# TensorE's four hardware loops written out as straight code, in a two-layer hybrid streaming encoder

## The reference

```
for layer in (0, 1):
    x += mixer(rmsnorm(x))             # layer 0: RG-LRU + sliding-window attention; layer 1: mLSTM
    h  = rmsnorm(x) @ ffn_w_in         # 1024 -> 2 * 2816
    x += (silu(h[:, :2816]) * h[:, 2816:]) @ ffn_w_out
    x += sigmoid(x @ ple_w_gate) * (p[layer] @ ple_w_proj)
y = rmsnorm(x)
```

## Time and profile before

| | |
|---|---|
| median of 3 runs | 2937.79 us (2936.8 to 2938.09) |
| the profiled execution's own time | 2937.61 us |
| its span | 2935.8 us |
| PE busy | 2762.8 us, 94% |
| PEld busy | 2692.7 us, 92% |
| DVE, POOL, ACT busy | 1270.1, 939.1, 603.6 us |
| share of PE in the chain that ended last | 87% |
| TensorE's granted clock, mean | 0.97 |

### The profile page before, as it was taken

How to read it: one execution, slowest core, us unless ns; L and a number is a source line. 1 busy time by engine, 2 the same in 40 slices (tenths; PEclk the granted TensorE clock), 3 DMA queues, 4 the chain that set the end, 5 groups by cost and what they waited for, 6 DMA issues and landing times.

```text
span 2935.8 us, 44303 instructions
## 1 busy us (share of the span) xinstructions
PE 2762.8 (94%) x17273; PEld 2692.7 (92%) x17273; DVE 1270.1 (43%) x2070; ACT 603.6 (21%) x1319; POOL 939.1 (32%) x439
## 2 busy tenths in 40 slices
PE   7999998999999999996999998789999999999996
PEld 5898888999999999996999987688999999999996
DVE  7835474323222223466834036647233332322465
ACT  4524322000000000133122135412100000000042
POOL 3222042333333333432434320023343333333430
PEclk9999999999999999998999999999999999999998
DMA  3101111111111111111212221311111111111111
GB/s 134 32 29 47 42 59 43 44 44 44 44 44 44 44 44 44 53 49 66 81 48 90 90 89 43 131 58 36 50 46 51 44 44 46 49 44 44 50 37 59
DMA packets 59752, 160.03 MB, mean 55 GB/s; under 512 B 9276, under 2 KB 30268, under 8 KB 58304
## 3 DMA queue, kind: packets, MB, share of 16 engines
q1 hardware_dynamic: 29952, 109.07, 12.2%
q10 hardware_dynamic: 29632, 48.42, 4.6%
HBM read 137.07 MB, written 20.40 MB: 54 GB/s over the span
## 4 chain that ended last, share of the span: by engine, by line
PE 87%; DVE 7%; ACT 3%; issue 2%; DMA 1%; ACTq 1%; POOL 0%; DVEq 0%; POOLq 0%
PE ps L394 27%; PE ps L395 27%; PE ps L396 27%; DVE tmp L915 1%; PE ps L784 1%; DVE rstd L866 1%; PE ps L821 1%; PE ps L566 1%; PE ps L596 1%; DVE xl L923 1%; DVE hb L1353 0%; PE ps L578 0%; DVE tmp L885 0%; PE ps L823 0%; PE ps L831 0%
## 5 line engine op out<-in xcount | busy, mean ns | idle before, releaser
L394 PE MATMUL ps<-xh,wh 128*128 128x352 f32 x3432 | 1128.0, 329 | 28.4 <-issue 14.2
L395 PE MATMUL ps<-xl,wh 128*128 128x352 f32 x3432 | 1119.1, 326 | 9.4 <-issue 9.4
L396 PE MATMUL ps<-xh,wl 128*128 128x352 f32 x3432 | 1118.8, 326 | 0.0
L436 POOL TENSOR_TENSOR wh<-raw,seeds 128x1024 fp32r<-128x1024 f32 x208 | 416.1, 2001 | 1911.1 <-PE ps L396 1905.3
L394 PEld LDWEIGHTS ps<-xh,wh 128*128 128x128 f32 x3432 | 655.9, 191 | 37.6 <-issue 16.0
L396 PEld LDWEIGHTS ps<-xh,wl 128*128 128x128 f32 x3432 | 655.4, 191 | 9.9 <-issue 9.9
L395 PEld LDWEIGHTS ps<-xl,wh 128*128 128x128 f32 x3432 | 655.4, 191 | 2.1 <-issue 0.8
L438 POOL TENSOR_TENSOR wl<-raw,wh 128x1024 fp32r<-128x1024 f32 x208 | 524.7, 2523 | 16.4
L999 DVE TENSOR_TENSOR tmpb<-ps,tmpa 128x352 f32<-128x352 f32 x132 | 69.0, 524 | 886.7 <-ACT tmpa L1492 886.7
L394 PE MATMUL ps<-hh,wh 128*128 128x352 f32 x1056 | 340.3, 322 | 0.0
L396 PE MATMUL ps<-hh,wl 128*128 128x352 f32 x1056 | 340.0, 322 | 0.0
(11 more groups left out here) (252 smaller groups left out, 2361.1 us busy)
## 6 DMA issues: line engine op xcount, KB each, us to landing
raw<-wstream SPq DMA_DIRECT2D x208, 512.0 KB, 3.5
vod<-stage ACTq DMA_DIRECT2D x72, 128.0 KB, 1.9
vb<-vod ACTq DMA_DIRECT2D x9, 512.0 KB, 4.0
ob<-vod ACTq DMA_DIRECT2D x9, 512.0 KB, 3.8
x<-xT ACTq DMA_DIRECT2D x3, 1408.0 KB, 8.8
x<-xT ACTq DMA_DIRECT2D x2, 2112.0 KB, 7.7
xsave<-x ACTq DMA_DIRECT2D x1, 4224.0 KB, 11.4
x<-xsave ACTq DMA_DIRECT2D x1, 4224.0 KB, 14.8
```

The lines of the kernel that those rows point to most:

```text
L394: pe.matmul(out, whi, mhi, start=first, stop=False)
L395: pe.matmul(out, whi, mlo, start=False, stop=False)
L396: return pe.matmul(out, wlo, mhi, start=False, stop=last)
L436: pool.tensor_tensor(hi, raw[:, r, :], zero, ALU.add).then_inc(hi_made, 1)
```

## The change

The four `with pe.Fori(a, b) as i` become `for i in range(a, b)`: the body is laid out once for each i when the program is built. Nothing else differs, and no other engine's program does.

```diff
             def dense_loop(phase, b0, nb, xl_at=None):
-                with pe.Fori(0, nb // NW) as i:
+                for i in range(0, nb // NW):
                     for j in range(NW):
...
                 up(c0, b0, b0 % NW, True)
-                with pe.Fori(0, FCH // 2) as i:
+                for i in range(0, FCH // 2):
                     for j in range(2):
                         cx = c0 + 2 * i + j
                         b = b0 + 4 + 6 * j + 12 * i
...
             for half in range(2):
-                with pe.Fori(0, 2) as i:
+                for i in range(0, 2):
                     for pr in range(2):
...
             chunk(0, None)
             front(1, P)
-            with pe.Fori(1, CH - 2) as i:
+            for i in range(1, CH - 2):
                 chunk(i, i - 1)
                 front(i + 1, i * P + P)
             chunk(CH - 2, CH - 3)
```

## The result

The changed kernel takes 2910.05 us (median of four runs, 2903.52 to 2911.93) against 2937.3 for the kernel before beside it (2934.97 to 2938.09): ratio 0.9905, 95% interval 0.9887 to 0.9922. That is 27 us less.

The account below looks back on a forecast made before the run. PE was taken as the bound, losing time at FFN back edges to instruction fetches and slow clock. 16.15 + 7.2 + 4.87 - 0.65 = 27.6 us off 2937.6 gave 2910.0, stated as 2910; range 2903 to 2916, some 88%.

Parts of the forecast that it names:

- Steps 1 and 2: Layer 0's FFN back edges: 16.15 us of PE idle time goes, and 7.2 us from the slow clock behind them.
- Steps 3 and 4: Layer 1's FFN back edges: 4.87 us of idle time goes, less 0.65 us for a faster spell lost.
- Step 4's rule: FFN iterations: faster spells come only after a pause; handovers without one lead to the slower pace; 0.65 us off the gain.
- step 3: Layer 1's back edges, 4.87 us: only the first packet is missing, a matter of where the code falls in memory.
- Step 5: PE's short branches and register instructions: removing them gains 0, as PE has matmuls queued meanwhile.
- Step 6: mLSTM: 0 gained, at most 3.7 us; its loop is slower through ACT's register work, and ACT's and DVE's loops stay.
- Straight code has to be fetched too: Rival: the other loops written out need some 13 more packets, 34 us if each held PE up: 2944; 3%.
- DVE's addition is what `up` waits for: Rival: the first gap at each FFN back edge stays, some 10 us in all: 2920; 4%.
- The clock stays low: Rival: the pauses go but 7.2 us of slow clock remain: 2917; 3%.

Follow-up runs that it names:

- the shifts: Kernel before with 24, 66, 8 (plus 64 ahead of the last mLSTM chunk), 16 or 34 waiting instructions ahead of layer 0's FFN: 2914.68, 2936.45, 2920.29, 2917.3, 2916.09 us.
- the swap: Kernel before with 66 waiting instructions ahead of layer 0's FFN, after which layer 1 had the long stalls and layer 0 the short: 2936.45 us, ratio 0.9999.

## Why the prediction was right

- *The total.* 2910 was forecast, 2910.05 measured. That they agree to a tenth is luck: runs of one kernel differ by several us. The trace answers for the terms.
- *Steps 1 and 2*, stalls and slow clock of layer 0: 16.15 + 7.2 = 23.35 forecast, 23.2 by the matmuls' starts. That the clock's part hangs on the length of the pause is borne out by the shifts: where one packet was missing PE paused for 0.9 to 2.2 us and kept full clock, where two were missing for 3.3 to 4.7 and lost it, in either layer.
- *Steps 3 and 4*: 4.87 - 0.65 = 4.2 forecast, 4.6 measured. The pauses were right; the loss was 0.3 and not 0.65, since the changed kernel's iterations take 139.12 us and not the 139.22 that the loss was reckoned from the earlier trace rows. Step 4's rule was also too simple: of layer 1's four pauses only the first was followed by a faster spell, and the first `up` of the changed kernel's loops has one with no pause at their start. That the short stall is a matter of where the code lies, said in step 3, is shown by the swap.
- *Step 5*: 0, and the kernel with the other loops written out is at 1.0002.
- *Step 6*: 0 from PE, right: the iterations stayed at 20.62. The reason was right in kind, the loops of ACT and DVE, and half wrong in name: the chain ran over ACT's L1856, but ACT's loop alone gave 0.1 of the 0.57.
- *The rivals.* "Straight code has to be fetched too": 137 packets in the whole kernel, 34 of them in layer 0's FFN loop, where PE has no gap at all. "DVE's addition is what `up` waits for": its waits vanished while DVE's program stayed the same; the view had named the last signal ahead of the pause. "The clock stays low": 1.00 from end to end of both FFN loops.
- *The Trainium skill.* "Runtime: NRT & Kernel Launch", section "Instruction fetch mechanics", gives 2,048 instructions held on TensorE and also a window of two pages for a taken branch. The traces side with the first: bodies of 886 instructions turn back free, one of about 1,810 can too when by the count it lies within eight packets, and it stalls when the ninth has been asked for. The prediction had set the figure of 2,048 aside because a body below it stalled; what it missed is that fetching ahead, not the body alone, uses up the room. As the sum was taken from the stalls themselves, this changed no number.

What stays open: what delays the request for the ninth packet. By my count of instructions, an estimate from two to a matmul of 0.16 us, PE's sequencer entered the eighth 1 to 4 us ahead of the branch with shifts of 8 to 34; the request came within about 1 us of that, or later, or not before the branch at all, differently from edge to edge of one execution.

## What to carry to other kernels

Look at the duration of the taken branches on each sequencer: in these traces 0.2 us means that the loop is held, 3 us and more that it is fetched again. PE's sequencer ran 2.6 us ahead of PE, so a branch of 3.6 us showed as a pause of only 1.2. Then the place of the loop's start in the packets decides between a pause of one to two microseconds and one of four with the clock behind it. Write out such a loop, or make its body clearly smaller than what is held (bodies of 886 instructions were held here; a smaller FFN body was not tried); shifting it by a few instructions won up to 22 of the 27 us, but changes with any edit ahead of it. PE's loops with short branches could stay as they were. Where a chain goes from engine to engine, as in the mLSTM, it can pay to write the loops out on the other engines it passes: 3.1 us here.

## What was unexpected of the hardware

- A hardware loop of some 1,810 instructions ran two iterations without an instruction packet; the same loop lying 16 instructions earlier paused at each turn.
- At the FFN's back edges pauses of up to 2.2 us left the clock at 1.00 every time; pauses of 3.3 to 4.7 us, with one matmul or none in them, were followed by 2.7 to 5.8 us of matmuls at half clock all 16 times that are in the traces.
- The same matmuls of 352 columns start 158.4 or 161.6 ns apart at full clock, in stretches of 8 us and more of one pace. In the changed kernel the first `up` of each FFN loop has stretches of 158.4, the nine others keep 161.6. In the kernel before the `up` behind the first of layer 1's pauses had them too, and those behind the other three had not. It was worth under 1 us in 45, and its cause wasn't looked for.
